# Strassen's seven products in the second layer's MLP, in quarters and with 256-row hand-overs to the down-projection

## The reference, cut to what matters

```python
def sq_relu_mlp(h, w_up, w_down):
    return jnp.square(jax.nn.relu(h @ w_up)) @ w_down
...
        xp = xp + mp[2] * op          # op = attention output @ w_o
        hp = pre_norm(xp, norm2_g[i], mp[3], mp[4])
        xp = xp + mp[5] * sq_relu_mlp(hp, mlp_up[i], mlp_down[i])
...
    y_prompt = rms_norm(xp, final_g)
```

## Time and profile before

| | |
|---|---|
| runs | 2817.85, 2813.07, 2817.62 us; median 2817.62 |
| profiled execution | span 2819.0 us; its own time is not given apart, it is 1.4 us above the median |
| busy in the span | TensorE 2631.8 us (93%), VectorE 1222.9 (43%), ScalarE 963.3 (34%), GpSimd 548.1 (19%) |
| second tail | from 1959.1 us, where the attention's last matmul starts, to the end; its last unit ends at 2803.49, the program at 2819.0 |

### The profile page before, as it was taken

How to read it: one execution, slowest core, us unless ns; L and a number is a source line. 1 busy time by engine, 2 the same in 40 slices (tenths; PEclk the granted TensorE clock), 3 DMA queues, 4 the chain that set the end, 5 groups by cost and what they waited for, 6 DMA issues and landing times. The chain is left out here.

```text
span 2819.0 us, 48837 instructions
## 1 busy us (share of the span) xinstructions
PE 2631.8 (93%) x20648; PEld 2480.1 (88%) x20648; DVE 1222.9 (43%) x2174; ACT 963.3 (34%) x1819; POOL 548.1 (19%) x348
## 2 busy tenths in 40 slices
PE   4989999989688999999999998987999999999998
PEld 3669888878578999999999998876989999999998
DVE  5358787269866211212212353766552122121223
ACT  5347632334444311202202342556342031121221
POOL 1022211123310222222221302111112222222230
PEclk7999999999889999999999999999999999999999
DMA  8878778798652222222222314111211111111121
GB/s 337 307 256 263 242 243 244 197 215 201 189 183 58 90 90 74 87 91 72 90 90 75 103 56 118 30 30 47 88 33 51 46 46 48 50 45 46 46 68 61
DMA packets 380913, 331.52 MB, mean 118 GB/s; under 512 B 113960, under 2 KB 350188, under 8 KB 373758
## 3 DMA queue, kind: packets, MB, share of 16 engines
q1 hardware_dynamic: 349804, 287.87, 33.7%
q10 hardware_dynamic: 25458, 21.57, 2.7%
q0 software_dynamic: 5440, 19.00, 1.8%
HBM read 248.27 MB, written 78.78 MB: 116 GB/s over the span
## 5 line engine op out<-in xcount | busy, mean ns | idle before, releaser
L547 POOL TENSOR_TENSOR wL<-raw,wH 128x1024 fp32r<-128x1024 f32 x120 | 288.2, 2402 | 1298.5 <-ACT wH L671 1298.5
L568 PE MATMUL t_acc<-oneH,wH 128*128 128x344 f32 x1488 | 483.2, 325 | 11.1 <-DVE oneL L915 5.0
L570 PE MATMUL t_acc<-oneH,wL 128*128 128x344 f32 x1488 | 477.9, 321 | 0.0
L569 PE MATMUL t_acc<-oneL,wH 128*128 128x344 f32 x1488 | 477.7, 321 | 0.0
L568 PE MATMUL t_acc<-twoH,wH 128*128 128x344 f32 x1392 | 449.0, 323 | 7.1 <-DVE twoL L890 4.8
L570 PE MATMUL t_acc<-twoH,wL 128*128 128x344 f32 x1392 | 445.6, 320 | 0.0
L569 PE MATMUL t_acc<-twoL,wH 128*128 128x344 f32 x1392 | 445.1, 320 | 0.0
L840 DVE SCALAR_TENSOR_TENSOR X<-t_acc,mod,X 128x344 f32<-128x344 f32 (+1 forms) x240 | 137.4, 572 | 612.5 <-PE t_acc L570 591.2
L920 DVE TENSOR_TENSOR t_g<-t_g 128x344 f32<-128x344 f32 x192 | 99.4, 518 | 553.4 <-ACT t_g L691 553.4
L568 PEld LDWEIGHTS t_acc<-oneH,wH 128*128 128x128 f32 x1488 | 281.6, 189 | 25.3 <-issue 10.1
L671 ACT ACTIVATE wH<-raw 128x1024 fp32r<-128x1024 f32 x120 | 126.7, 1056 | 507.5 <-PE t_acc L570 507.5
(11 more groups left out here) (473 smaller groups left out, 4732.7 us busy)
## 6 DMA issues: line engine op xcount, KB each, us to landing
raw<-in_mlp_down SPq DMA_DIRECT2D x64, 512.0 KB, 4.0
raw<-in_mlp_up SPq DMA_DIRECT2D x62, 512.0 KB, 4.1
ada_ring<-in_ada_w SPq DMA_DIRECT2D x24, 1024.0 KB, 7.6
shared<-in_ada_w SPq DMA_DIRECT2D x24, 1024.0 KB, 6.2
kvrb_hx<-hx_saved ACTq DMA_DIRECT2D x16, 516.5 KB, 4.3
kvr_work<-scr_L SPq DMA_DIRECT2D x16, 516.0 KB, 6.0
X<-x_saved SPq DMA_DIRECT2D x6, 1376.0 KB, 7.3
raw<-in_at_wqkv SPq DMA_DIRECT2D x12, 512.0 KB, 3.9
```

The source lines that it names most:

```text
L547: pool.tensor_tensor(low, raw_of(w), high.bitcast(F32), ALU.subtract).then_inc(s_low, 1)
L568: pe.matmul(out, high[:, k, :], h[:, k, third[t]], start=(k == 0), stop=False)
L569: pe.matmul(out, high[:, k, :], l[:, k, third[t]], start=False, stop=False)
L570: return pe.matmul(out, low[:, k, :], h[:, k, third[t]], start=False, stop=(k == DB - 1))
```

## The change

The first layer's tail stays `stage_tail`; the second layer gets a stage of its own, `stage_last`.

- Tokens are cut in four quarters of 258 columns; quarters 0 and 1 form token half p=0, quarters 2 and 3 half p=1. The "o" projection becomes 32 units of 24 matmuls with 258 columns.
- The up-projection of two inner blocks (a pair, 16 of them) for one token half is a 2x2 block product: weights halved in inner block and in input features, tokens halved in input features and in quarters. It is computed by seven products instead of eight, each of 12 matmuls (four blocks, high and low) with 258 columns. Its operands are sums of blocks: the token sums (four of the seven operands) are made once and kept on chip with high and low parts (`combined`, three areas of SBUF, over which "one" and "two" lay before), the weight sums are made by GpSimd in each round (four instructions of 128x512).
- The results of products are added on the way out: P6, P7 and P4 run on in one bank, P5 and P3 in another, P1 and P2 in a third; VectorE adds them to what it kept (`after_p6` to `after_p3`), applies ReLU and square, and writes low parts.
- 20 rounds: pairs 0 to 3 for half 0, the same for half 1, then pairs 4 to 15 for both halves. In each round, between P1, P2 and the five others, the down-projection of the round before stands: two inner blocks (K = 256), units of 6 matmuls, added to X at once. A round of one half has 7 products and 16 units of 258 columns, a round of both has 14 products and 24 units of 344.
- Weights come in units of 128x512 through a ring of four: seven for the products, four for the down-projection, ScalarE high and GpSimd low for each.
- Quarter 3's normalisation and the sums and splits for half 1 are spread over rounds 0 to 3 (`fills`), on VectorE and ScalarE.
- The last down-projection goes by thirds, with the output tiles between its units as before.

```diff
@@ -208,18 +208,19 @@
             with stage(net):
                 stage_scan(net)
         net.X = sb("X", [128, DB, TOK])
-        one = [sb(f"one{n}", [128, DB, TOK], F32R) for n in "HL"]
         net.wH = sb("wH", [128, 2, DB, 128], F32R)
-        for layer in range(2):
-            if layer == 1:
-                net.HH, net.HL = one
+        with ExitStack() as plain:
+            one = [plain.enter_context(nc.sbuf_tensor(f"one{n}", [128, DB, TOK], F32R)) for n in "HL"]
+            with ExitStack() as pair:
+                two = [pair.enter_context(nc.sbuf_tensor(f"two{n}", [128, DB, TOK], F32R)) for n in "HL"]
+                (net.HH, net.HL), (net.GH, net.GL) = two, one
                 with stage(net):
-                    stage_attention(net)
-            with ExitStack() as pair:
-                two = [pair.enter_context(nc.sbuf_tensor(f"two{n}{layer}", [128, DB, TOK], F32R)) for n in "HL"]
-                (net.HH, net.HL), (net.GH, net.GL) = (one, two) if layer else (two, one)
-                with stage(net):
-                    stage_tail(net, layer)
+                    stage_tail(net, 0)
+            net.HH, net.HL = one
+            with stage(net):
+                stage_attention(net)
...
+PROLOGUE = 4
+PAIRS = FF_GROUPS * DB // 2
+FIRST, REST = ("P1", "P2"), ("P6", "P7", "P5", "P4", "P3")
+PRODUCTS = FIRST + REST
...
+def mlp_rounds():
+    half = [[(j, (p,)) for j in range(PROLOGUE)] for p in range(2)]
+    pairs = half[0] + half[1] + [(j, (0, 1)) for j in range(PROLOGUE, PAIRS)]
+    return [(j, ps, pairs[r - 1] if r else None) for r, (j, ps) in enumerate(pairs)]
...
+    def add_down(r, pair, ps, wide):
+        spans = ranges_of(ps)
+        for i in range(4):
+            weights.append(("d", r, i))
+        units = [(m, s) for s in spans for m in range(DB)] if wide else [(m, s) for m in range(DB) for s in spans]
+        for n, (m, s) in enumerate(units):
+            mid_bank[len(jobs)] = n
+            ends["d", r, m // 2] = len(jobs)
+            jobs.append(("d", r, m, pair, s))
...
+    for r, (pair, ps, mid) in enumerate(rounds):
+        for name in FIRST:
+            weights.append(("p", r, name))
+            for p in ps:
+                ends["p", r, name] = len(jobs)
+                jobs.append(("p", r, name, p))
+        at = len(jobs)
+        if mid:
+            add_down(r, *mid, False)
+        mids.append((at, len(jobs)))
+        for name in REST:
+            weights.append(("p", r, name))
+        for names in [(name,) for name in REST[:3]] + [REST[3:]]:
+            for p in ps:
+                for name in names:
+                    ends["p", r, name] = len(jobs)
+                    jobs.append(("p", r, name, p))
+    mids.append((len(jobs), len(jobs) + NT * DB))
+    add_down(R, rounds[-1][0], (0, 1), True)
+    weight_at = {what: w for w, what in enumerate(weights)}
...
+    SPREAD = {1: (0,), 2: (1, 2), 3: (3,), 4: (4,), 5: (5,), 6: (6,), 7: (7,)}
+    SUMS = {(2, 3): (0, 2), (2, 4): (2, 4), (2, 5): (4, 7), (2, 6): (7, 10), (2, 7): (10, 12), (3, 0): (12, 16)}
+    LATER = 8 + 16 + 28
+    fills = []
+    for r in range(PROLOGUE):
+        fills += [(r, "d", n, 1) for n in range(1, 2 * DB, 2) if r] + [(r, x, 0, n) for x, n in (("P6", 2 if r else 0), ("P7", 2), ("P5", 2), ("P3", 3))]
+    step_at, s = {}, 0
+    for i, (r, x, n, k) in enumerate(fills):
+        step_at[r, x, n] = (i, min(s, LATER), min(s + k, LATER))
...
+            def load_up(r, half, second):
+                n = 2 * half + second
+                if r:
+                    sp.wait_ge(s_low, weight_at["p", r - 1, ("P7", "P3", "P5", "P4")[n]] + 1)
+                col = (2 * rounds[r][0] + half) * 128
+                w = up[second * 512:second * 512 + 512, col:col + 128].rearrange("(k p) m -> p k m", p=128)
+                sp.dma_start(raw_unit(n).rearrange("p (k m) -> p k m", k=4), w).then_inc(s_unit[n], 16)
+            def load_down(r, i):
+                pair = rounds[r - 1][0]
+                if i == 0:
+                    sp.wait_ge(s_low, weight_at["p", r - 1, "P6"] + 1)
+                elif i == 1:
+                    if r > 1:
+                        sp.wait_ge(s_low, weight_at["d", r - 1, 3] + 1)
+                else:
+                    sp.wait_ge(s_low, weight_at["d", r, i - 2] + 1)
+                w = down[2 * pair * 128:(2 * pair + 2) * 128, i * 256:(i + 1) * 256].rearrange("(k p) m -> p k m", p=128)
+                sp.dma_start(raw_unit(4 + i % 2).rearrange("p (k m) -> p k m", k=2), w).then_inc(s_unit[4 + i % 2], 16)
+            out_panel(4)
+            out_panel(5)
+            load_x(0)
+            out_panel(6)
+            out_panel(7)
+            load_x(1)
+            sp.wait_ge(s_olow, 6)
+            for half in range(2):
+                for second in range(2):
+                    load_up(0, half, second)
+            load_x(2)
+            load_x(3)
+            sp.wait_ge(s_done, 3 * DB)
+            for r in range(1, R):
+                load_down(r, 1)
+                load_down(r, 0)
+                load_up(r, 0, 0)
+                load_up(r, 1, 0)
+                load_up(r, 1, 1)
+                load_up(r, 0, 1)
+                load_down(r, 2)
+                load_down(r, 3)
...
+            def low(w):
+                pool.wait_ge(s_high, w + 1)
+                high, to = slot(w)
+                pool.tensor_tensor(to, raw_unit(unit_of(weights[w])), high.bitcast(F32), ALU.subtract).then_inc(s_low, 1)
...
+            for r, (_, _, mid) in enumerate(rounds):
+                low(weight_at["p", r, "P1"])
+                pool.wait_ge(s_unit[2], 16 * (r + 1))
+                pool.tensor_tensor(q11, q11, q21, ALU.subtract).then_inc(s_wsum, 1)
+                pool.wait_ge(s_unit[3], 16 * (r + 1))
+                pool.tensor_tensor(q21, q21, q22, ALU.add).then_inc(s_wsum, 1)
+                low(weight_at["p", r, "P2"])
+                if mid:
+                    for i in range(3):
+                        down_low(r, i)
+                    pool.wait_ge(s_low, weight_at["d", r, 2] + 1)
+                else:
+                    pool.wait_ge(s_done, 3 * DB)
+                pool.wait_ge(s_wsum, 4 * r + 1)
+                pool.tensor_tensor(extra, q22, q11, ALU.subtract).then_inc(s_wsum, 1)
+                if mid:
+                    down_low(r, 3)
+                pool.wait_ge(s_wsum, 4 * r + 3)
+                pool.tensor_tensor(q12, q12, extra, ALU.subtract).then_inc(s_wsum, 1)
+                for name in REST:
+                    low(weight_at["p", r, name])
+            for i in range(4):
+                down_low(R, i)
...
+            def bank_free(r, n):
+                at, end = mids[r]
+                busy = [u for u in range(at, end) if mid_bank[u] % 4 == n]
+                pe.wait_ge(s_add, added[busy[-1]] if busy else 3 * DB + 5 + n)
...
+            def product(u):
+                _, r, name, p = jobs[u]
+                w, n, c = weight_at["p", r, name], turn[r, p], PRODUCTS.index(name)
+                pe.wait_ge(s_low, w + 1)
+                if name == "P1":
+                    out = lead[p]
+                    if before[r, p] is not None:
+                        pe.wait_ge(s_r11, turn[before[r, p], p] + 1)
+                elif name == "P2":
+                    out = lead[p]
+                    pe.wait_ge(s_p1, n + 1)
+                elif name == "P6":
+                    out = acc[p]
+                    bank_free(r, p)
+                elif name == "P7":
+                    out = acc[p]
+                    pe.wait_ge(s_u2, n + 1)
+                elif name == "P5":
+                    out = acc[2 + p]
+                    bank_free(r, 2 + p)
+                elif name == "P4":
+                    out = acc[p]
+                    pe.wait_ge(s_u3, n + 1)
+                else:
+                    out = acc[2 + p]
+                    pe.wait_ge(s_c22, n + 1)
+                high, low = (x.rearrange("p (k m) -> p k m", k=4) for x in slot(w))
+                fresh = name in ("P1", "P6", "P5")
+                for i in range(4):
+                    if r in (0, PROLOGUE):
+                        pe.wait_ge(s_cl, 28 * p + 4 * c + i + 1)
+                    ins = three(out[:, 0:TQ], high[:, i, :], low[:, i, :], combined(p, c, i, 0), combined(p, c, i, 1), fresh and i == 0, i == 3)
+                ins.then_inc(s_done, 1)
...
+            def hidden(u):
+                _, r, m, _, (a, z) = jobs[u]
+                w, n = weight_at["d", r, m // 2], mid_bank[u]
+                s, ps = r - 1, rounds[r - 1][1]
+                pe.wait_ge(s_low, w + 1)
+                blocks = range(a // TQ, (z - 1) // TQ + 1)
+                pe.wait_ge(s_gl, max(piece_at[s, q // 2, x] for q in blocks for x in (("11", "21"), ("12", "22"))[q % 2]) + 1)
+                if n < 4:
+                    pe.wait_ge(s_c21, turn[s, ps[-1]] + 1)
+                    pe.wait_ge(s_c12, turn[s, ps[-1]] + 1)
```

(109 more changed lines are left out.)

444 lines of the change are left out of this document (added).

## The result

The changed kernel takes 2876.0 us (median of 4 runs, 2868.1 to 2877.9) against 2816.1 for the one before (median of 4, 2813.1 to 2817.9): ratio 1.021, 95% interval 1.0196 to 1.0229. I had forecast 2807, with a range of 2782 to 2844. Its profiled execution has a span of 2875.9 us at a mean clock of 0.963 and a time of its own of 2877.7.

A forecast was written before the change was run, and what follows sets the result against it. TensorE was taken as the bound: 2819.0 less 43.1 for matmuls, plus 25.4 of other losses and 7 at the end gave 2808.3 us profiled, 2807 as median. Own range 2790 to 2825; with rivals 2782 to 2844.

The forecast's parts named there:

- Matmuls, 0.118: Second tail: each 258-column matmul costs 0.118 us, so all matmuls come to 769.2 us, 43 us less.
- the other half covers each hand-over: Rounds 9 to 19: no engine but TensorE is the bound; 0.2 us lost per round, 2.2 in all.
- I cost both at nothing: All rounds: SP's additional loads and ScalarE's 11 high copies a round (9 us of 21) add no time.
- The lock, 0.3 us a wait: VectorE instructions with two SBUF inputs exclude GpSimd's work, each waiting 0.3 us on average.
- Rounds 1 to 3, 11.5: The lock sets these rounds: 4.5 us over TensorE's time twice, 2.5 in round 3, 11.5 us lost.
- 4 to 8, 8.7: One-half rounds: uncovered hand-overs and P1's late copy lose 2 us a round four times, 0.7 in round 8.
- No stall: Rounds 4 to 8: GpSimd readies P2's weights in some 8.5 of 8.7 us, with nothing to spare.
- Quarter 3, 9: End of the "o" stage: VectorE needs 35 us against TensorE's 25.5, so the third mean square waits 9 us.
- round 0, 8.5: Round 0, without a down-projection to cover it: P1's copy comes late on VectorE's list and lock, 8.5 us lost.
- Entry and transposes, 17: Start of "o": first window's loss of 10 us stays, plus 7 for four mean squares and transposes among units.
- the end, 7 more: After the last unit: 23 us of output where 15.5 were, taken as 7 us more.
- the lock costs twice: Rival, chance 0.27: locked instructions wait 0.6 us instead of 0.3 in quarter 3 and rounds 0 to 8; 2839 us.

The follow-up runs named there:

- e1: Changed kernel with GpSimd's low parts of weights and three of four weight sums per round cut to 8 of 512 columns: 2816.6 us.
- e6: Changed kernel with pieces kept in PSUM, ReLU and squares on ScalarE, VectorE's lows reading one PSUM input: 2840.2 us, ratio 1.0092.
- e3: e2 plus, on ScalarE, the last half's high parts of pieces 21 and 12 behind the next P1's copy from round 5 on: 2856.1 us.
- e2: Changed kernel with P1's copy going into two places in turn for each token half, ScalarE's order unchanged: 2877.6 us.
- e4: Changed kernel with GpSimd's lows and sums of MLP weights moved to VectorE: 2880.1 us, ratio 1.0215.
- e10: e6 and e5 combined, P1's copy ahead of old pieces and fill steps on ScalarE, VectorE's early fill steps behind P3, quarter 3's inverse root in PSUM: 2814.5 us.
- e5: Changed kernel with ScalarE's three combined highs ahead of square and normalisation in each unit of quarter 3: 2876.5 us.
- e11: e10 with quarter 3's X reload in two halves, the first asked for half a quarter earlier: 2809.3 us, ratio 0.9979.
- e8: Changed kernel with ScalarE's fill steps behind P3 of rounds 0 to 2 moved behind the next P1's copy: 2872.2 us.

## Why the prediction was wrong

The forecast was 2808.3 on the profiled execution; the span after is 2875.9. The 67.6 between them: matmuls 9.7, losses 58.2 (115.8 against 57.6), 2.5 from the tail's later start, and 2.8 the other way at the end (19.7 behind the last matmul where I had 22.5).

- **Matmuls, 0.118.** Measured 0.1203: 778.9 in place of 769.2. I had "0.121 if it is a fixed addition" beside it and took the other from a difference of 4 ns in listed lengths, which overlap and are no start-to-start. The gain in matmuls is 33 us, not 43.
- **Rounds 9 to 19, "the other half covers each hand-over".** This is the step that failed by most in its kind: 2.2 forecast, 21.7 measured. I compared sums of busy time with 42 us (VectorE 24, GpSimd 17.4) and found no bound. But P2 waits for a copy that stands in ScalarE's order behind two pieces, and these behind VectorE's locked squares. The cover for that hand-over is the other half's P1, 1.44 us; one locked instruction takes 0.9 of it. e1 and e6 show the lock (21.7 to 0.9 and 3.7), e3 the order (1.8 to 0.5 a round), e2 that it isn't the place, and e4 that VectorE's own work ahead of the hand-over would have cost as much (19.5).
- **"ScalarE: ... I cost both at nothing".** Its load is indeed small (123 of 492 us). Its order is not free: that was the sentence to work out.
- **The lock, 0.3 us a wait.** As an average of all rounds it was right (0.21 to 0.30), but not where it mattered most: 0.56 in rounds 4 to 8. Right was also that squares are locked, as the Trainium skill (SBUF — State Buffer, "SBUF: two separate sides") has it by its count of ports; that an input from PSUM frees an instruction is shown by e6. Wrong was GpSimd's 1.16, where 1.29 (alone, e6) to 1.51 were measured, and, above all, to charge the waits to VectorE's sum. On a chain of hand-overs they come in whole.
- **Rounds 1 to 3, 11.5, and 4 to 8, 8.7.** Measured 27.8 and 24.7. For rounds 4 to 8 e1 gives 7.3: my count of hand-overs was good and GpSimd's long instructions came on top, 17.4 where I had charged 2.4. I had two locks of 0.3 us ahead of P1's copy; in round 6 three locked instructions stand there, two squares of 1.07 and 1.05 and a low of 1.49, 2.3 us of waiting in all against 0.6. "No stall" for P2's weights was too good as well: in rounds 5 to 7 their low part comes 0.8 us late, hidden behind the copy, and in e3 it sets P2's start. For 1 to 3 e1 gives 13.3, so half of the loss comes with GpSimd's long instructions; e10 gets to 14.7 with all of GpSimd's work, by order (and by the squares' move to ScalarE). Whether the rest is order or work no run shows.
- **Quarter 3, 9, and round 0, 8.5.** Measured 5.7 and 20.7, in all 26.4 against 17.5. I had 35 us for VectorE against 25.5. The ping-pong with ScalarE, 1.0 us a unit, was not in it; e5 removes it, 6 us. The X wait, 3.85, was (as 4); e11 shows it to be worth 4 in quarter 3.
- **Entry and transposes, 17, last hand-over, 0.7; the end, 7 more.** 8.9 in the first three quarters and 6.2 among the last units, where the transposes stand: 15.1, about right. Behind the last matmul 19.7 where 15.5 were, 4.2 more; my own terms for it gave 8.2 (38.8 less 15.1 less 15.5), of which I took 7.
- **Small readings.** The columns fall by 5.6%, not 5.7, and a round has 8 loads of 256 KB, not 11. Neither enters the sum.

Of my rivals, "the lock costs twice" has the sign and most of the stages (not quarter 3), and its 2839 was the nearest. Its condition, a mean wait of over 0.5 us, was met in rounds 4 to 8 (0.56) and not elsewhere (0.34 and 0.19). So it was partly right about the rate. But most of the miss is the place of the waits: even where the rate was below my 0.3, in rounds 9 to 19, the loss was 21.7, for which the rival had 5 more than my 2.2.

**Still open:** the 6.5 to 8.4 us in round 0, for which nothing was tried with less work in quarter 3; and how much of the losses is the low clock. In round 0 the clock is 0.74, and matmuls behind the long wait start 0.21 us apart (2083.47, 2083.68, 2083.90 in the timeline) instead of 0.12. In the whole tail 150 short matmuls start some 0.21 apart and 12 long ones some 0.28, about 15 us more than at the full clock, but no run separated this from the waits that go before.

## What to carry to other kernels

Where engines hand results on in a ring, don't compare sums of busy time: follow one hand-over through the program order of every engine it passes, and ask what stands ahead of it there and whether that can be locked. Read waits by stage, not as one mean. The lock was removed here by where operands lie (one input from PSUM, 36 us), and not by moving GpSimd's work to VectorE, which cost as much as the lock. Deferrable work belongs behind the instruction that feeds TensorE, on all the engines of the chain at once; changing one link alone gave back 3 us of loss or none (e2, e5, e8).

## What the runs showed of the hardware

- Matmuls of 258 columns, each with its own weights, start 0.1203 us apart, those of 344 columns 0.1567: 0.42 ns a column and 13 ns fixed.
- An operation x·x whose inputs are the same SBUF tensor waits for GpSimd as one with two tensors does (1.34 us against 0.43). VectorE's instructions with one input from PSUM don't (0.43 inside a GpSimd instruction of 1.29, e6), nor do ScalarE's squares (0.39 at 2118.73 in e10, inside two of GpSimd's).
- The lock slows GpSimd too: its 128x512 instructions take 1.29 to 1.30 us in e6, where from round 4 on little on VectorE competes, and 1.32 to 1.51 in the changed kernel (means of groups).
- Under back-to-back GpSimd work a VectorE instruction can wait for most of a GpSimd one, however short it is itself: in e11 three that take 1.10 together at 2052.91, with GpSimd idle, take 4.20 at 2045.48, and one of 8 columns takes 1.05 at 2054.51.
